# Fused streaming encoder step: dense operands of 544 token columns, with the convolution gap kept in the convolution buffers only

## What is computed

```python
def causal_dwconv(x, hist, w):                     # width 3, per channel
    xp = concatenate([hist, x], axis=1)            # two rows of history in front
    return sum(w[j] * xp[:, j:j + T] for j in range(3)), xp[:, -2:]

h = rmsnorm(x, g1); z = h @ w_in                   # 1024 -> 8200 columns
mq, mk, mv, mo, mi, mf, sb, sc, sx, dq, dk, dv, gt = split(z)
ya = sigmoid(mo) * rmsnorm(mlstm(mq, mk, mv, mi, mf))        # branch A
cu, conv_state = causal_dwconv(sc * sx, hist, sc_w); yb = sb * cu   # branch B
yc = rmsnorm(differential_attention(dq, dk, dv))             # branch C
x = x + (sum over b of sigmoid(gt[b]) * (y[b] @ w_br[b])) @ w_o
up = rmsnorm(x, g2) @ w_up                         # 1024 -> 5632
upc, ffn_state = causal_dwconv(up, fhist, f_w)
x = x + (silu(upc[:, :2816]) * upc[:, 2816:]) @ w_dn
y = rmsnorm(x, norm_f)
```

## Time and profile before

| | us |
|---|---|
| median of 3 runs | 1071.81 |
| lowest, highest run | 1070.44, 1072.72 |
| span of the profiled execution, first to last instruction | 1066.9 |
| PE busy (matmul) | 1035.0 |
| DVE busy | 516.5 |
| ACT busy | 349.4 |
| POOL busy | 180.8 |

### The profile page before, as it was taken

The page is one execution under the profiler, slowest core; times in us unless marked ns, Lnnn a source line. Parts: engine busy times, 40 slices in busy tenths (PEclk is TensorE's granted clock), DMA queues, the critical chain, the costliest instruction groups (busy, mean ns, idle before and its releaser), DMA issues.

```text
span 1066.9 us, 19010 instructions
## 1 busy us (share of the span) xinstructions
PE 1035.0 (97%) x8074; PEld 1008.7 (95%) x8074; DVE 516.5 (48%) x712; ACT 349.4 (33%) x616; POOL 180.8 (17%) x360
## 2 busy tenths in 40 slices
PE   5999999989999999999999999999999999999996
PEld 4999899988988999999999999999999999999996
DVE  6443343323344446333334445777777777533232
ACT  5333233323344433222223333343333333322121
POOL 4001222200222212200012120112112111111010
PEclk8999999989999999999999999999999999999998
DMA  6223214371202042221513222233222232332212
GB/s 184 79 80 89 80 41 122 107 222 41 79 2 88 32 119 80 80 80 41 158 45 106 88 92 67 80 99 100 80 79 80 80 95 80 101 87 82 82 56 84
DMA packets 93451, 92.45 MB, mean 87 GB/s; under 512 B 3492, under 2 KB 86329, under 8 KB 93367
## 3 DMA queue, kind: packets, MB, share of 16 engines
q1 hardware_dynamic: 88559, 82.09, 25.2%
q10 hardware_dynamic: 3784, 6.29, 1.9%
q0 software_dynamic: 1024, 2.86, 0.9%
HBM read 86.15 MB, written 5.08 MB: 86 GB/s over the span
## 4 chain that ended last, share of the span: by engine, by line
PE 93%; DMA 2%; DVE 2%; ACT 1%; POOL 1%; issue 0%; ACTq 0%; DVEq 0%
PE D L1314 85%; DMA ck<-in_cache_k 1%; PE X L1496 1%; PE X L1532 1%; DVE hn_x L1040 1%; PE X L1466 1%; PE X L1501 1%; ACT tmp L730 0%; PE D L1399 0%; PE X L1444 0%; PE X L1443 0%; PE X L1428 0%; PE X L1446 0%; DMA x_t<-in_x_prompt 0%; PE X L1515 0%
## 5 line engine op out<-in xcount | busy, mean ns | idle before, releaser
L1314 PE MATMUL D<-h_h,w_h 128*128 128x274 f32 (+1 forms) x1744 | 367.4, 292 | 7.6 <-DVE h_l L1034 5.5
L1314 PE MATMUL D<-h_h,w_l 128*128 128x274 f32 (+1 forms) x1744 | 366.3, 291 | 0.0
L1314 PE MATMUL D<-h_l,w_h 128*128 128x274 f32 (+1 forms) x1744 | 364.6, 290 | 0.0
L984 DVE TENSOR_TENSOR w_l<-raw,w_h 128x1024 fp32r<-128x1024 f32 (+3 forms) x172 | 196.8, 1145 | 197.4 <-ACT w_h L751 192.6
L1314 PEld LDWEIGHTS D<-h_h,w_h 128*128 128x128 f32 (+1 forms) x1744 | 275.6, 189 | 10.6 <-issue 4.5
L1314 PEld LDWEIGHTS D<-h_l,w_h 128*128 128x128 f32 (+1 forms) x1744 | 276.5, 189 | 0.4
L1314 PEld LDWEIGHTS D<-h_h,w_l 128*128 128x128 f32 (+1 forms) x1744 | 276.3, 189 | 0.4
L751 ACT ACTIVATE w_h<-raw 128x1024 fp32r<-128x1024 f32 (+3 forms) x172 | 162.2, 944 | 107.7 <-PE D L1314 79.5
L952 ACT ACTIVATE acc<-ups,fcw 128x548 f32<-128x548 f32 x44 | 33.2, 755 | 168.5 <-POOL ffn_last L697 168.5
L1314 PE MATMUL D<-g_h,w_h 128*128 128x274 f32 x352 | 73.9, 291 | 0.9 <-issue 0.9
L1314 PE MATMUL D<-g_h,w_l 128*128 128x274 f32 x352 | 73.8, 291 | 0.0
(11 more groups left out here) (323 smaller groups left out, 1107.1 us busy)
## 6 DMA issues: line engine op xcount, KB each, us to landing
raw<-in_w_in SPq DMA_DIRECT2D x32, 1024.0 KB, 5.7
raw<-in_w_up SPq DMA_DIRECT2D x22, 1024.0 KB, 5.1
raw<-in_w_down SPq DMA_DIRECT2D x16, 704.0 KB, 4.5
raw<-in_w_branch SPq DMA_DIRECT2D x6, 1024.0 KB, 5.0
raw<-in_w_out SPq DMA_DIRECT2D x4, 1024.0 KB, 5.2
x_t<-in_x_prompt SPq DMA_DIRECT2D x4, 512.0 KB, 5.6
ck<-in_cache_k ACTq DMA_DIRECT2D x1, 2048.0 KB, 14.8
cv<-in_cache_v ACTq DMA_DIRECT2D x1, 2048.0 KB, 22.6
```

The costliest lines, as they stand in the source:

```text
L984: v.tensor_tensor(lo, src, hi.bitcast(F32), ALU.subtract).then_inc(S["wl_ready"], 1)
L1314: last = t.matmul(banks(n)[0:w.shape[2], half, 0:HALF], w[:, k, :], x[:, kx, HALF * half:HALF * half + HALF], start=kx == 0 and i == 0, st ...
```

## The change

The gap leaves all operands of matmuls: `S0 = TP`, `T = 544`, `HALF = 272`. The convolution's buffers and their results keep the gap, now of two columns as far as it is read, in rows of `TW = T + 4 = 548`. Results that lie dense in PSUM (two halves of 272) are put into a gapped row by two instructions in place of one: `gapped` gives first the columns 0 to 239 of both halves, then columns 240 to 271, of which the second half's are the 32 sample tokens. The last product of the "up" stage, which goes back to a dense row, is split at the gap too. The memsets of the gap go, and with them two semaphore waits. The diff, cut to its core:

```diff
-S0 = TP + 4
+S0 = TP
 T = S0 + TS
 HALF = T // 2
+CUT = HALF - TS
+TW = T + 4
...
-        tmp = place("tmp", [P, 2, T])
+        tmp = place("tmp", [P, 2, TW])
...
-        u_c = place("u_c", [P, 2, T + 2], K_AT)
+        u_c = place("u_c", [P, 2, TW + 2], K_AT)
-        scb = place("scb", [P, 4, T], WORK_AT)
+        scb = place("scb", [P, 4, TW], WORK_AT)
-        ups = place("ups", [P, 2, T + 2], FF_AT)
-        acc = place("acc", [P, 2, 2, T], FF_AT + up32(8 * (T + 2)))
+        ups = place("ups", [P, 2, TW + 2], FF_AT)
+        acc = place("acc", [P, 2, 2, TW], FF_AT + up32(8 * (TW + 2)))
...
+        def gapped(row, dense):
+
+            for cols, wide in ((slice(0, CUT), T), (slice(CUT, HALF), TW)):
+                yield two(row[:, 0:wide])[:, :, cols], dense[:, :, cols]
...
-            g.memset(xT[:, :, TP:S0], 0.0).then_inc(S["const_ready"], 1)
...
-                elif kind == "at" and a[0] == 0 and a[1] == 1:
-
-                    for y in (yc_h, yc_l):
-                        last = g.memset(y[:, :, TP:S0].bitcast(F32), 0.0)
-                    last.then_inc(S["yc_spare"], 1)
...
-                    sc.activation(acc[:, part, j % 2, :], ups[:, m % 2, 2:T + 2], ACT.Copy, scale=fcw[:, 2, jj:jj + 1])\
+                    sc.activation(acc[:, part, j % 2, 0:T + 2], ups[:, m % 2, 2:T + 4], ACT.Copy, scale=fcw[:, 2, jj:jj + 1])\
...
-                    v.memset(rstd[0][:, TP:S0], 0.0)
...
-                    if r == 1:
-                        v.memset(rstd[1][:, TP:S0], 0.0)
...
-                    v.tensor_tensor(two(u[:, 2:T + 2]), dbuf(n), two(scb[:, j, :]), ALU.mult)\
-                        .then_inc(S["dve_drained"], 1)
+                    for (to, d), (_, c) in zip(gapped(u[:, 2:], dbuf(n)), gapped(u[:, 2:], two(scb[:, j, 0:T]))):
+                        last = v.tensor_tensor(to, d, c, ALU.mult)
+                    last.then_inc(S["dve_drained"], 1)
...
-                    v.tensor_tensor(two(tmp_of(("sb", a[0]))), dbuf(n), two(scb[:, a[0], :]), ALU.mult)\
-                        .then_inc(S["dve_drained"], 1)
+                    for (cu, d), (_, to) in zip(gapped(scb[:, a[0], :], dbuf(n)),
+                                                gapped(scb[:, a[0], :], two(tmp_of(("sb", a[0]))))):
+                        last = v.tensor_tensor(to, d, cu, ALU.mult)
+                    last.then_inc(S["dve_drained"], 1)
...
-                    v.tensor_tensor(two(u[:, 2:T + 2]), dbuf(n), two(rstd[1]), ALU.mult)\
-                        .then_inc(S["dve_drained"], 1)
+                    for (to, d), (_, r) in zip(gapped(u[:, 2:], dbuf(n)), gapped(u[:, 2:], two(rstd[1]))):
+                        last = v.tensor_tensor(to, d, r, ALU.mult)
+                    last.then_inc(S["dve_drained"], 1)
...
-                        v.tensor_tensor(acc[:, 0, j % 2, :], acc[:, 0, j % 2, :], ac, ALU.mult)\
+
+                        v.tensor_tensor(s[:, 0:TP], s[:, 0:TP], ac[:, 0:TP], ALU.mult)
+                        v.tensor_tensor(s[:, S0:T], s[:, TP + 2:T + 2], ac[:, TP + 2:T + 2], ALU.mult)\
                             .then_inc(S["g_ready"], 1)
```

More of the change, by code:

```diff
@@ L301, in streaming_encoder_step @@
         ssum = {1: place("ssum1", [P, T], DK_AT), 2: place("ssum2", [P, T], H_AT)}
-        rstd = [place("rstd0", [P, T], DK_AT)[:], tmp[:, 1, :]]
+        rstd = [place("rstd0", [P, T], DK_AT)[:], tmp[:, 1, 0:T]]
         f_tmp = place("f_tmp", [P, 2, T], M_AT)
@@ L309, in streaming_encoder_step @@
         bd_u = place("bd_u", [36, H, P], M_AT + 8 * T + 4 * 2560, F32R)
-        bd_i = place("bd_i", [36, H, P], TMP_AT + up32(4 * T), F32R)
+        bd_i = place("bd_i", [36, H, P], TMP_AT + up32(4 * TW), F32R)
         rows_t = place("rows", [H, 8, T], G_AT)
@@ L334, in streaming_encoder_step @@
         wdT = place("wdT", [P, 9, P], K_AT + 16384 + 8448)
-        u_c = place("u_c", [P, 2, T + 2], K_AT)
-        yc_l = place("yc_l", [P, 4, T], K_AT + up32(8 * (T + 2)), F32R)
-        A_AT = K_AT + up32(8 * (T + 2)) + 16 * T
+        u_c = place("u_c", [P, 2, TW + 2], K_AT)
+        yc_l = place("yc_l", [P, 4, T], K_AT + up32(8 * (TW + 2)), F32R)
+        A_AT = K_AT + up32(8 * (TW + 2)) + 16 * T
         on = place("on", [P, 2, P], A_AT)
@@ L352, in streaming_encoder_step @@
         FF_AT = M_AT + 8 * JF * T
-        ups = place("ups", [P, 2, T + 2], FF_AT)
-        acc = place("acc", [P, 2, 2, T], FF_AT + up32(8 * (T + 2)))
-        ffn_last = place("ffn_last", [P, 2, 2, JU], FF_AT + up32(8 * (T + 2)) + 16 * T)
-        assert FF_AT + up32(8 * (T + 2)) + 16 * T + 16 * JU <= END_AT
+        ups = place("ups", [P, 2, TW + 2], FF_AT)
+        acc = place("acc", [P, 2, 2, TW], FF_AT + up32(8 * (TW + 2)))
+        ffn_last = place("ffn_last", [P, 2, 2, JU], FF_AT + up32(8 * (TW + 2)) + 16 * TW)
+        assert FF_AT + up32(8 * (TW + 2)) + 16 * TW + 16 * JU <= END_AT
         Y_AT = H_AT + 2 * up32(4 * T)
@@ L388, in streaming_encoder_step @@
                 "lam_dve lam_act "
-                "y_v y_h y_split yc_split yc_spare "
+                "y_v y_h y_split yc_split "
                 "u_ready conv_kept "
@@ L417, in tmp_of @@
         def tmp_of(key):
-            return tmp[:, tmp_slot[key], :]
+            return tmp[:, tmp_slot[key], 0:T]
         def banks(n):
@@ L724, in _ @@
             act.dma_start(x_s[0:TS, :], x_sample[0]).then_inc(S["xs_in"], 16)
-            act.wait_ge(S["const_ready"], 8)
+            act.wait_ge(S["const_ready"], 7)
             for c, (_, L) in enumerate(TILES):
@@ L754, in high_g @@
                 act.wait_ge(S["g_ready"], j + 1)
-                sc.activation(g_h[:, j, :], acc[:, 0, j % 2, :], ACT.Copy).then_inc(S["gh_ready"], 1)
+                sc.activation(g_h[:, j, :], acc[:, 0, j % 2, 0:T], ACT.Copy).then_inc(S["gh_ready"], 1)
             for g in range(AHEAD):
@@ L956, in _ @@
                         wait_tmp_free(act, ("up", j))
-                        sc.activation(tmp_of(("up", j)), acc[:, 0, j % 2, :], ACT.Tanh, scale=0.5)\
+                        sc.activation(tmp[:, tmp_slot[("up", j)], 0:T + 2], acc[:, 0, j % 2, 0:T + 2], ACT.Tanh, scale=0.5)\
                             .then_inc(S["th_ready"], 1)
@@ L1086, in _ @@
                     v.tensor_scalar(row["lf"], row["lf"], b_f[:], None, ALU.add).then_inc(S["rows_dve"], 1)
-                    v.memset(row["inter"][:, TP:S0], 0.0)
                     link(v.memset(row["em"], 1.0))
@@ L1264, in _ @@
                     m = up_index[a]
-                    u, ac = ups[:, m % 2, :], acc[:, part, j % 2, :]
+                    u, ac = ups[:, m % 2, :], acc[:, part, j % 2, 0:T + 2]
                     dve.wait_ge(S["dense_done"], n + 1)
@@ L1357, in _ @@
                     if c == 0:
-                        pe.wait_ge(S["const_ready"], 8)
+                        pe.wait_ge(S["const_ready"], 7)
                     pe.wait_ge(x_in[c] if c < 4 else S["xs_in"], 16)
@@ L1383, in _ @@
                             pe.wait_ge(S["yc_split"], 17)
-                            pe.wait_ge(S["yc_spare"], 1)
                     product(n, (ya_h, yb_h, yc_h)[br], (ya_l, yb_l, yc_l)[br])
@@ L1439, in _ @@
                             wait_drained(pe, block_of[("tok", ("mv", 3))])
-                            pe.wait_ge(S["const_ready"], 9)
+                            pe.wait_ge(S["const_ready"], 8)
                         for h in hs:
```

30 lines of the change are left out of this document (16 added, 14 removed).

## The result

| us | before | after |
|---|---|---|
| median of the runs | 1071.12 (4 runs) | 1055.24 (4 runs) |
| lowest, highest | 1070.04, 1072.72 | 1053.62, 1055.69 |
| span of the profiled execution | 1066.9 | 1053.9 |

A forecast was written before the change was run, and what follows sets the result against it. PE's dense matmuls were taken to bound the kernel. Columns -6.4, lost gains +0.15, the change to "dn" +0.25, memsets and shorter elementwise work -0.1 gave -6.1 us: 1071.81 to 1065.7 us, range 1057.5 to 1072.5.

The forecast's parts named there:

- What bounds the kernel: Whole kernel: PE's dense products of L1314, 85% of the chain's span; time is matmul count times the 127.6 ns step.
- What the step is made of: Dense matmuls: 13.4 ns above the columns' 114.2, not load or issue but operand reading or PSUM writing, scaling or fixed.
- The columns' term: Dense matmuls: two columns fewer save 0.88 ns each, 6.4 us over 7248 matmuls.
- Rival 1: Dense matmuls' operand reads: rounder addresses speed them beyond the columns, to 1054.8 or 1058.7 us; chance 0.20.
- Its stronger form: Second halves come down to the first, 3 ns for 3624 matmuls, 10.9 us beyond the forecast: 1054.8 us; chance 0.10.
- Its weaker form: Halves touch 68 stretches of 16 bytes, not 69: 1.85 ns a matmul, 13.4 us, 1058.7 us; half of 0.20.
- The sign that it named: Dense pairs: the halves, 126 and 129 ns before, become equal if the address counts.
- Rival 2: Dense matmuls: something independent of columns sets 127.6 ns at full clock, nothing gained, 1072.0 us; chance 0.15.
- Rival 3: Dense matmuls: rounder addresses slow reads to 128.2 ns a step, 4.3 us more, 1076.2 us; chance 0.08 with rival 4.
- The drains: DVE's PSUM drains in two instructions: 0.12 us more each, 9 us of DVE work with the last products, no time lost.
- The place at the change to "dn": End of "up": both added instructions lie on the path before PE starts "dn", 0.25 us more (0.1 to 0.4).
- What doesn't reach the end: Matmul gains lost in PE's waits: 0.1 us at the key cache, 0.06 before 921.98 us, together 0.15 us.

The follow-up runs named there:

- the table: Changed kernel and kernel before, some up and down blocks reading other widths and starts; up-block steps 118.4 to 132.8 ns; executions 1056.13 and 1063.93 us.
- the first experiment: Changed kernel with the second half of every dense product read from column 270 in place of 272: 1071.13 us, ratio to the kernel before 1.001.
- the first trace: Profiled execution of the changed kernel in the original measurement: span 1053.9 us, median of the runs 1055.24 us.
- the second: Second trace of the changed kernel, unaltered and run again beside the kernel before: median 1055.06 us, ratio 0.9861.

## Why the prediction was wrong

**What bounds the kernel** was right. Every view that held before holds after, and all the gain came from one line's step.

**What the step is made of** was half right. The load and the issue were rightly struck out, and what was left, the reading of the operand, is what moved. "Either scales with the columns or carries a fixed part beside them" is the step that failed: it left out that the time can go by stretches of 16 bytes. Of the 2.48 ns that a step lost, two columns as columns would be 0.88; one stretch less (69 to 68) is 1.75 by the table. The other 0.7 ns is of the kind that pairs of starts differ by, and is open. So is most of the first experiment's 16 us: half a stretch is 0.9 of its 2.8 ns. That the reading's place in units of 16 bytes sets the step is shown; the whole rule isn't. The Trainium skill, "SBUF — State Buffer", section "Specifications (TRN2)", says that SBUF has lines of 16 bytes and that each crossing to a new line pays a penalty. The traces agree in kind, with 1.75 ns for each further stretch.

**The columns' term** was therefore mis-sized: 0.88 ns a matmul for a measured 2.48, 6.4 us for 17.6 us in the trace.

**Rival 1** was the one that came, with a chance of 0.20. Its stronger form gave 1054.8 us, and 1055.24 were measured; but the range had been cut so that just this form lay outside, on the ground of its chance alone. That the two times lie so near is luck in part. The form had 17.3 us from the step and 0.3 us given back, where the trace shows 17.6 and 4.7; what brings the sums together is that the medians differ by 2.9 us more than the two traced executions. Its mechanism wasn't the right one either: it brought the second half down to the first by its start. The start alone, put right with 274 columns, gave nothing (ratio 0.9996). Its weaker form had the right mechanism as far as that is known, and 13.4 us, too little by 0.6 ns a step. The sign that it named, equal halves, did come: 125.4 and 125.1. "No row is nearer to one than to the other" was true of the two slopes; the difference of the halves, 3 ns, was a row against both, and it should have had more weight than 0.20.

**Rivals 2 and 3.** Rival 2 is out by the 20 us of the kernel before with 272 columns. Rival 3 wanted a step of 128.2 ns and got 125.2; in the table of widths the rows of 2176 bytes are no slower than those of 2192 (0.1 ns faster as a mean). What did cost 16 us was the less round address, in the first experiment.

**The drains** were priced too high, and it didn't matter. DVE's groups in the stage of "up" (count, busy us, mean ns, idle before; as the earlier trace rows):

```profile
L1275 DVE TENSOR_TENSOR ups<-D,tmp 128x480 f32<-128x480 f32 x44 | 28.6, 650 | 0.0
L1291 DVE TENSOR_TENSOR acc<-acc 128x512 f32<-128x512 f32 x22 | 15.2, 692 | 0.8
L1275 DVE TENSOR_TENSOR ups<-D,tmp 128x64 f32<-128x64 f32 x44 | 9.4, 214 | 0.0
L1292 DVE TENSOR_TENSOR acc<-acc 128x32 f32<-128x32 f32 x22 | 4.1, 185 | 0.0
```

A pair of 650 and 214 ns overlaps: merged in the timeline it takes 0.78 us, where the single one took 0.72. So 0.06 us a drain, not 0.12, and DVE's busy time in a stretch of 272 us went from 202.1 to 206.0 us, not to 209. Through the whole stage PE had no wait in "up", as was said.

**The place at the change to "dn"** was the right place and the wrong size: 0.25 us said, 0.94 measured (the distance from start to start went from 1.17 to 2.10 us). The chain behind the last drain grew by 0.1 us only, from 9.28 (913.57 to 922.85) to 9.38 us (903.25 to 912.63). But the drain itself began late. The timeline of DVE after:

```profile
902.41 0.18 DVE L1292 TENSOR_TENSOR acc<-acc 128x32 f32<-128x32 f32 x1
902.51 0.82 DVE L985 TENSOR_TENSOR w_l<-raw,w_h 128x640 fp32r<-128x640 f32 x1
903.25 0.78 DVE L1275 TENSOR_TENSOR ups<-D,tmp 128x480 f32<-128x480 f32 x2
```

and before:

```profile
912.41 0.82 DVE L984 TENSOR_TENSOR w_l<-raw,w_h 128x640 fp32r<-128x640 f32 x1
913.57 0.73 DVE L1273 TENSOR_TENSOR ups<-D,tmp 128x548 f32<-128x548 f32 x1 [0.34 <-PE D L1314]
```

PE began "dn" at 902.36 us after, 913.37 before. In the kernel before DVE had 0.34 us to spare at this drain; in the changed one it came 0.7 us late: PE's blocks had become 0.12 us shorter each while DVE's work had become longer. 0.7 + 0.1, and 0.17 for PE's 66 faster matmuls ahead of the wait, make about the 0.94. The kernel before with fast halves and its old drains had 1.34 us there, so PE's speed without the added instructions gives only 0.2 of it. The hold that the prediction feared there changed nothing: L1282 took 1.89 us before and its successor 1.90 after. The others don't all take 0.73 us, as the prediction read; in both traces half of the 22 take 0.72 and half 1.9.

**What doesn't reach the end** was too small at the key cache as well: 0.1 us said, 1.5 in the first trace and 0.9 in the second, most of it in the length of the transfer, which the prediction had left as it was.

**Not foreseen:** a stretch at the lower clock near 125 us, in all five traces with the fast halves and the new drains (3.4 us long). It is not in the kernel before, nor in that kernel with fast halves, nor in the changed kernel with its second half off by 8 bytes. It follows a run of small matmuls. The distances there are 1.5 us longer for it (0.7 between dense products, 0.8 between small ones). Whether it goes with the change or with where in time that run falls can't be told by these traces.

## What to carry to other kernels

Before pricing an operand by its columns, find what the step is above the columns at full clock, and look whether equal instructions differ by where they read; a difference that sits on one of two halves is a sign that the layout is being paid for. Here halves that begin and end on multiples of 16 bytes took 2.5 ns off a step where two columns had been priced at 0.9. And when the bounding engine gets faster, look for the places where another engine was in time by a few tenths of a microsecond: the stall comes back there.

## What the runs showed of the hardware

A run of float32r matmuls with 128 x 128 weights, a load each, at a granted clock of 1.00, has a step of 118.4 ns at 256 columns and 132.5 at 288 (up blocks, halves from 0 and 256). It goes up by some 1.75 ns for each further stretch of 16 bytes that the moving operand touches in a partition, and follows this count to within 0.57 ns, against 0.96 for the columns. A start 16 or 32 bytes off a multiple of 64 cost nothing (124.8 to 125.4 ns). A second half 8 bytes off cost 0.3 ns (0/274, 272 columns) to 2.8 ns (0/270 in the changed kernel), and both halves 4 bytes off 3 ns in the up blocks and 0.5 in a down block. At a clock of 0.50 the step was the columns times one cycle of 1.2 GHz, before and after. The steps repeat to a fraction of a nanosecond from block to block, and yet the down blocks of the changed kernel take 124.4, 125.0 or 126.1 ns with the same form; what picks one of the three is open.
